# Gate products placed between the last sparse values and the mLSTM weights; another place for half of a branch's weights

## The reference, cut to what matters

```
z = rms(x) @ w_in                       # q, k, v of three mixers, and g_pre
y_a = sigmoid(m_o) * rms(mlstm(...))    # branch 0
y_b = dsa(...)                          # branch 1: sparse attention, top 64 keys
y_c = rms(diff_attn(...))               # branch 2
gates = sigmoid(g_pre + b_gate)         # 3 x 1024 columns of z
merged = sum(gates[b] * ((y_a, y_b, y_c)[b] @ w_branch[b]) for b in (0, 1, 2))
x = x + merged @ w_out
x = x + swiglu(rms(x))
```

## Time and profile before

| | |
|---|---|
| median of 3 runs | 2477.12 us |
| lowest, highest run | 2474.83, 2484.95 us |
| span of the profiled execution | 2479.3 us |
| PE, DVE, ACT busy | 99%, 75%, 63% |
| chain that ended last | PE 92%, DVE 3%, DMA 2%, ACT 1% |

### The profile page before, as it was taken

How to read it: one execution, slowest core, us unless ns; L and a number is a source line. 1 busy time by engine, 2 the same in 40 slices (tenths; PEclk the granted TensorE clock), 3 DMA queues, 4 the chain that set the end, 5 groups by cost and what they waited for, 6 DMA issues and landing times.

```text
span 2479.3 us, 30443 instructions
## 1 busy us (share of the span) xinstructions
PE 2449.2 (99%) x12028; PEld 2044.3 (82%) x12028; DVE 1850.2 (75%) x1856; ACT 1552.6 (63%) x1892; POOL 29.8 (1%) x36
## 2 busy tenths in 40 slices
PE   8999999999999999999999999999999999999998
PEld 8788888897887889978888997888888888788886
DVE  6877744478776546645545578999999999999998
ACT  5675543457565444365444447788878787878886
POOL 0000000000000000010000000000000000000001
PEclk9999999999999999999999998999999999999999
DMA  7444655354435565675555556999999999999996
GB/s 251 152 136 153 221 182 175 132 175 158 135 137 205 202 212 170 207 252 192 198 203 179 162 195 268 392 364 401 376 394 374 398 380 388 390 374 394 372 391 252
DMA packets 183223, 637.96 MB, mean 257 GB/s; under 512 B 11196, under 2 KB 52594, under 8 KB 139914
## 3 DMA queue, kind: packets, MB, share of 16 engines
q1 hardware_dynamic: 179562, 622.87, 68.3%
q0 software_dynamic: 3488, 12.59, 1.3%
HBM read 616.54 MB, written 18.88 MB: 256 GB/s over the span
## 4 chain that ended last, share of the span: by engine, by line
PE 92%; DVE 3%; DMA 2%; ACT 1%; issue 1%; SPq 0%; DVEq 0%; ACTq 0%
PE bank L561 88%; DVE split L2142 2%; PE bank L598 2%; PE bank L903 1%; DMA ring<-in_moe_w_gate 1%; DMA ring<-in_moe_w_up 1%; ACT split L1529 1%; ACT parts L1529 0%; DVE parts L2211 0%; PE bank L1449 0%; DVE oT_high L2156 0%; DVE parts L2122 0%; DMA const<-in_tables 0%; DVE x_resid L2184 0%; DVE tmp L2199 0%
## 5 line engine op out<-in xcount | busy, mean ns | idle before, releaser
L561 PE MATMUL bank<-split,parts 128*128 128x512 f32 (+1 forms) x6432 | 1467.4, 388 | 6.2 <-DVE parts L2211 1.8
L561 PEld LDWEIGHTS bank<-split,parts 128*128 128x128 f32 x6432 | 1186.6, 188 | 253.6 <-issue 15.2
L1529 ACT ACTIVATE split<-ring 128x2048 fp32r<-128x2048 f32 x444 | 848.7, 1922 | 441.6 <-PE bank L561 411.9
L2142 DVE TENSOR_TENSOR split<-ring,split 128x2048 fp32r<-128x2048 f32 x444 | 994.0, 2283 | 59.8 <-ACT split L1529 59.4
L2211 DVE TENSOR_TENSOR parts<-bank,parts 128x512 fp32r<-128x512 f32 x128 | 82.4, 686 | 159.0 <-ACT parts L1529 157.5
L1529 ACT ACTIVATE halves<-ring 128x1024 fp32r<-128x1024 f32 x96 | 101.0, 1061 | 129.9 <-PE bank L561 129.4
L2156 DVE TENSOR_TENSOR halves<-ring,halves 128x1024 fp32r<-128x1024 f32 x96 | 116.1, 1224 | 73.0 <-ACT halves L1529 72.3
L561 PE MATMUL bank<-ring_low,z_high 128*128 128x512 f32 (+2 forms) x384 | 146.9, 382 | 0.0
L561 PE MATMUL bank<-xparts,halves 128*128 128x256 f32 x960 | 116.4, 283 | 0.0
L561 PEld LDWEIGHTS bank<-xparts,halves 128*128 128x128 f32 x960 | 115.5, 192 | 0.5 <-DVE xparts L2122 0.2
L561 PE MATMUL bank<-z_high 128*128 128x512 f32 (+3 forms) x304 | 111.0, 365 | 0.0
(11 more groups left out here) (342 smaller groups left out, 2335.2 us busy)
## 6 DMA issues: line engine op xcount, KB each, us to landing
ring<-in_moe_w_gate SPq DMA_DIRECT2D x112, 1024.0 KB, 8.2
ring<-in_moe_w_up SPq DMA_DIRECT2D x112, 1024.0 KB, 7.7
ring<-in_moe_w_down SPq DMA_DIRECT2D x112, 1024.0 KB, 7.8
ring<-in_w_gate_up SPq DMA_DIRECT2D x44, 1024.0 KB, 5.9
ring<-in_w_in SPq DMA_DIRECT2D x40, 1024.0 KB, 5.2
ring<-in_ret_w_in SPq DMA_DIRECT2D x24, 1024.0 KB, 5.3
ring<-in_w_down SPq DMA_DIRECT2D x22, 1024.0 KB, 7.0
ring<-in_w_in SPq DMA_DIRECT2D x20, 880.0 KB, 4.8
```

The lines of the kernel that those rows point to most:

```text
L561: return nc.tensor.matmul(o, l, r, start=first, stop=final, **kw)
L1529: return nc.scalar.activation(out, in_, func, **kw)
L2142: V.tensor_tensor(split[:, split_place(m), 1, :], ring[:, n % RING, :], split[:, split_place(m), 0, :].bitcast(F32), ALU.subtract).then_in ...
```

## The change

On PE, the first unit of gate 0 is begun after the fifth batch of sparse values (j = 4) and no longer after the turned heads. After each of its eight `mm3` a piece of other work is issued: the last sparse values (j = 5), floor and exponents 0, exponents 1, and then four times the weights of a head (with the exponents of head h + 2 behind it). The banks of the sparse values are kept out of the turn meanwhile, as the gate banks are. The high part of `b11` goes to place E in place of D, and that of `g01` to D in place of E; ACT makes the high parts of `b10` and `b11` one step earlier each, and DVE their low parts: `b10` after `g00`, and `b11` behind the mLSTM weights and ahead of `branch_lows(1)`. What is computed is the same.

```diff
-           "g1": "E H A2 E", "b1": "A2 D", "g0": "H E A2 H", "g2": "A2 D E H", "b0": "G D", "b2": "H B"}
+           "g1": "E H A2 E", "b1": "A2 E", "g0": "H D A2 H", "g2": "A2 D E H", "b0": "G D", "b2": "H B"}
...
@@ split_chunk, after each mm3
+                            if between is not None:
+                                next(between, None)
...
+                def sparse_values(j):
...
+                for j in range(5):
+                    turn_probs(j + 1)
+                    if j != 1 and j < 4:
+                        next(between)
+                    if j in (0, 2):
+                        bo[j // 2] = fill(ALL)
+                        open_banks.add(bo[j // 2])
+                    sparse_values(j)
                 next(between, None)
-                point("dsa")
-                mlstm_weights()
+
+                def last_values_and_weights():
+                    sparse_values(5)
+                    point("dsa")
+                    yield
+                    yield from mlstm_weights()
+
+                ahead = last_values_and_weights()
+                first_gates = gate_tiles(0, ahead)
+                next(first_gates)
+                for _ in ahead:
+                    pass
                 eng.wait_ge(dve_freed.sem, pe.point("dsa", dve_freed))
                 turn_branch(True)
                 turn_heads(lambda tt, c: zc(tt, C_DQ + c, P), lambda tt, c: zc(tt, C_DK + c, P))
                 place_free["D"] = [(for_act, for_act.marked)]
-                first_gates = gate_tiles(0)
-                next(first_gates)
                 mlstm_values()
...
@@ mlstm_weights
                 exponents(0)
+                yield
+                exponents(1)
+                yield
                 for h in range(4):
-                    if h < 3:
-                        exponents(h + 1)
                     b = fill(ALL)
...
                     point("weights")
+                    if h < 2:
+                        exponents(h + 2)
+                    yield
...
@@ ACT
                     if j == 4:
+                        column_highs("b10")
                         gate_tiles(1)
-                column_highs("b10")
+                column_highs("b11")
...
-                column_highs("b11", "g01", "g02", "g03")
+                column_highs("g01", "g02", "g03")
...
@@ DVE
-                        column_lows("g00")
+                        column_lows("g00", "b10")
...
                 mlstm_weights()
+                column_lows("b11")
                 branch_lows(1)
-                column_lows("b10", "b11")
                 mlstm_values()
```

More of the change, by code:

```diff
@@ L785, in mix_part, with split_chunk @@
                 return low_in[0][:, k // 4, k % 4, :] if i else xs_high[:, k // 4, k % 4, :]
-            def split_chunk(n, chunk, bias=None):
+            def split_chunk(n, chunk, bias=None, between=None):
                 b = [fill(ALL) for _ in range(TT)]
@@ L1065, in columns, with gate_tiles @@
                     point(name)
-                def gate_tiles(branch):
+                def gate_tiles(branch, between=None):
                     for i in range(2):
-                        yield from split_chunk(512, f"g{branch}", bias=6 * li + 2 * branch + i)
+                        yield from split_chunk(512, f"g{branch}", bias=6 * li + 2 * branch + i, between=between)
                     point("gates")
@@ L1185, in layer @@
                 turn_probs(0)
-                for j in range(6):
+                bo = {}
+                def sparse_values(j):
                     tt, _, hs = score_bank(j)
[L1188 to L1193, removed]
                     eng.wait_ge(act_freed.sem, pe.point("pT", act_freed))
@@ L1197, in layer @@
                             c = (i * (tt + 1) + s) * P
-                            ins = mm(bank[bo][:, h * HD:(h + 1) * HD], pT[:, j % 2, c:c + P],
+                            ins = mm(bank[bo[tt]][:, h * HD:(h + 1) * HD], pT[:, j % 2, c:c + P],
                                      kv[:, s, HALF + h * HD:HALF + (h + 1) * HD], s == 0, s == tt)
                     if j in (1, 5):
-                        hand(ins, bo, "dve")
-                next(between, None)
-                point("dsa")
-                mlstm_weights()
+                        hand(ins, bo[tt], "dve")
+                        open_banks.discard(bo[tt])
+                for j in range(5):
[6 more added lines that the diff above has]
+                    sparse_values(j)
+                next(between, None)
+                def last_values_and_weights():
[8 more added lines that the diff above has]
+                    pass
                 eng.wait_ge(dve_freed.sem, pe.point("dsa", dve_freed))
```

## The result

| | median | lowest to highest | ratio to before, 95% interval |
|---|---|---|---|
| before | 2480.12 us (7 runs) | 2474.83 to 2484.95 | |
| after | 2489.68 us (7 runs) | 2487.07 to 2491.75 | 1.0036 [1.0025, 1.0046] |

The changed kernel is slower, by 0.36% or some 9 us, above the range that was forecast (2471.5 to 2482). An execution takes 1.8 us more than its span (2489.55 against 2487.8 for the profiled one), so the profiled execution of before stands for 2481.1 us.

A forecast was written before the change was run, and what follows sets the result against it. PE, busy 99% of the span, was taken to bound the kernel, with a clock fall in the first layer. -3.25 plus 1.36 of costs gave -1.9 us, so 2475.2 from a median of 2477.1; range 2471.5 to 2482.

The forecast's parts named there:

- The turned branch: At `mlstm_values`, nothing now stands between to cover DVE's low part: PE waits 0.25 us, bounds 0 and 2.28.
- the sum: Over both layers: -3.25 for the clock plus 2 x (-0.22 + 0.65 + 0.25), giving -1.9 us.
- These cost nothing: Place E for `b11`, `g01` in D, SP's order and `g00`'s ring slot were claimed to add no time.
- The clock, first layer: Large products among the small work from 168 to 180 us prevent the clock's fall: -3.25 us, bounds -3.25 and 0.
- The wait for `pT`: At the sparse values of j = 5, bias and gate products now cover ACT's copy: -0.22 us a layer.
- Passing between kinds: Interleaving large and small products on PE costs 1.40 in place of 0.75: +0.65 us a layer, bounds +0.05 and +1.4.
- The unknown pass: Large work behind a 4-row operand, four times a layer, not in the trace: taken as 0.15 us each, bounds 0 and 0.33.
- The wait of the first value: PE stands at the first mLSTM value until DVE has made the branch's low part: +0.25 us a layer.
- The range: The forecast's own range with the bounds of the unknown costs was 2472.5 to 2478 us; the range given was wider.
- the one on the other side: The clock falls anew in transposes and `mlstm_values`, 5.1 us of small work: 2478.5 to 2481.7 us, chance 0.13.
- The first rival: The median's runs had no clock fall, so only costs remain: 2478.5 us; chance 0.27, shared with a fall that stays.

The follow-up runs named there:

- 1: The changed kernel, with the first chunk's two banks kept out of the turn while gate 0's second chunk takes its banks: 2478.39 us, 0.9994 of before.
- 5: As 1, but on DVE the low part of `b11` stands behind `branch_lows(1)` instead of ahead of it: 2475.91 us, 0.9983 of before.
- 8: As 5, but gate 0's first unit is issued in one piece behind the values of j = 4, not interleaved: 2477.7 us, 0.9986 of before.
- 6: As 5, but the four exponents are issued in two pairs behind the floor, ahead of all weights: 2476.12 us, 0.9984 of before.
- 2: The kernel before, with gate 0's second chunk taking banks 1 and 2 in place of 4 and 5: 2497.98 us, 1.0073 of before.
- 7: The changed kernel, with four throwaway products issued into the free first bank ahead of PE's wait for the second: 2485.66 us, 1.0019 of before.

## Why the prediction was wrong

For the stretch that I worked out, the terms came out nearly as summed. The step that failed is "The turned branch", at its end and in the sum: there I followed the turn of the PSUM banks up to the mLSTM values and took all behind `split_branch(1)` as it was before ("These cost nothing"). I did not ask which banks the second chunk of gate 0 would get. It got a bank just handed to ACT, and PE stood 4.15 us for it in each layer.

- The clock, first layer, -3.25: right in outcome. It is 1.00 over the stretch in both layers, in 1 and 5 as well. That the large products between small ones keep it up is not shown: 8 has none between them and no run under 0.996, and 6 has them and fell in both layers. Over 35 runs of before the mean clock is 0.993 to 0.996, over 12 of 5 it is 0.996 or 0.997.
- The wait for `pT`, -0.22: as priced. The values of j = 5 begin at 170.40 and pace 0.81 for eight.
- Passing between kinds, +0.65: right. 5, which has no wait, takes 19.20 - 18.80 = +0.40 for the stretch, and without the -0.22 for `pT` that leaves +0.62. Within it errors cancel. The unknown pass, large behind a 4-row product, was 0.34 in place of 0.23, +0.11 where I took 0.15. But the last large product ahead of a 4-row one also took 0.33 (173.52 to 173.85 below), which I had not counted, and two heads' weights behind large products took 0.57 against 0.705 in a row.

```profile
172.95 0.50 PE L561 MATMUL bank<-heads_high,z_high 128*128 128x512 f32 x1
173.29 0.39 PE L561 MATMUL bank<-ring_low,z_high 128*128 128x512 f32 x1
173.52 0.40 PE L561 MATMUL bank<-heads_high,oT_high 128*128 128x512 f32 x1
173.85 0.69 PE L561 MATMUL bank<-ybuf,const 4*128 4x256 f32 x2
```

- The wait of the first value, +0.25: PE is idle for 0.21, but 5, which takes the wait away, is 0.45 a layer shorter. From the transposes of the heads to the first value it is 2.12 us against 1.74 in 5, and the values themselves take 2.67 against 2.60. So the idle time that the profile shows is about half of what this wait cost. Timeline of PE, kernel after:

```profile
183.21 1.91 PE L598 MATMUL bank<-const,z 128*128 128x128 f32 x16
185.33 2.92 PE L561 MATMUL bank<-v_ext,pbuf 128*128 128x129 f32 x24 [0.21 <-DVE ybuf_tmp_high L2634]
188.00 0.47 PE L561 MATMUL bank<-z_high,ybuf_tmp_high 128*128 128x512 f32 x1
```

- What the sum left out: a wait of 4.15 us and a fall of the clock of 2.3 to 2.4 us, twice, for 13.7 us with the small differences of those stretches. 1 removes it, 2 makes it, 7 parts it. The sign against the sum's -1.9 follows.
- The range: the sum's own bounds (+0.05 and +1.4 for the passes, 0 and 2.28 for the wait) give 2473.5 to 2480.8 with the clock kept, not the 2472.5 to 2478 that I wrote. Neither holds the result.
- The rivals: the one on the other side looked for a fall of the clock in the new stretch of small work; that stretch kept 1.00. A fall came where PE was idle. The first rival was half right: the mean clocks of before go from 0.993 to 0.996, as they would if it ran both with and without a fall. But its median over more runs lies at 2480, and 22 of 35 runs have a mean clock below that of every run of 5, so a fall seems to belong to its usual run. And I compared the profiled execution's span with a median of times: with the 1.8 us between the two it stood 4.0 over that median, not 2.2.

With the banks mended, 1 measured 2.1 us under before, where the sum said 1.9. That closeness is luck: the interval of 1 takes in no change, and the stretches of the profiled executions give -2.34 + 0.85 = -1.5. Clear of before are only the kernels that have no wait at the values as well (5, 6 and 8), by 2 to 4 us.

## What to carry to other kernels

Where buffers are given out in turn, moving a piece that holds two of them open shifts who gets which buffer for everything behind it, so after such a move list, for each later taking, the bank and its last reader, and ask when that reader runs, down to the next piece of the same kind. A short wait on the engine that sets the time costs more than its length if the clock falls in it; here 4.15 us cost 2.3 more. When the profile of a moved stretch is as predicted and the time is not, follow the start times of both kernels onward until their distance jumps.

## What the runs showed of the hardware that was not expected

An idle PE of 4.15 us cost 2.3 to 2.4 us more in the work behind it: products 0.42 us apart at a granted clock of 0.50, until 214.0. With 3.6 us of that wait filled by products whose results are thrown away, the clock kept 1.00. And the clock fell, to 0.61 over 3.5 us, in a stretch in which PE was busy all the time (6, in both layers), as it had in before's first layer (0.52 over 7.1 us); what brings on these falls is open. A wait that the profile shows as 0.21 us idle cost 0.45 (5 against 1).
